# Expert rows gathered as 64 tokens by two picks, with their sums on the two column halves of TensorE's array

## The reference

```python
def peer_sublayer(h, g_ffn, w_peer_q, keys_1, keys_2, peer_u, peer_v):
    x = rmsnorm(h, g_ffn).reshape(-1, shape[-1])
...
    v1, i1 = lax.top_k(s1, PEER_TOPK)
    v2, i2 = lax.top_k(s2, PEER_TOPK)
    cand = (v1[..., :, None] + v2[..., None, :]).reshape(T, PEER_HEADS, PEER_TOPK * PEER_TOPK)
    sc, ci = lax.top_k(cand, PEER_TOPK)
...
    eidx = (e1 * PEER_NKEYS + e2).reshape(T, PEER_HEADS * PEER_TOPK)
    gates = jax.nn.softmax(sc, axis=-1).reshape(T, PEER_HEADS * PEER_TOPK).astype(x.dtype)
...
    def block(args):
        xt, it, gt = args
        act = jax.nn.gelu(jnp.einsum('td,tkd->tk', xt, peer_u[it]), approximate=False)
        return jnp.einsum('tk,tkd->td', gt * act, peer_v[it])
```

## Time and profile before

| | us |
|---|---|
| median of 3 runs | 2607.19 |
| lowest, highest | 2602.67, 2608.74 |
| span of the profiled execution | 2607.3 |
| first fetch issued | 661.6 |
| last product of the gather (`Y`) starts | 2033.7 |
| PE, DVE, ACT, POOL busy | 2152.8, 1647.3, 1003.4, 702.4 |
| bytes moved by the gather's queue | 536.90 MB |

### The profile page before, as it was taken

How to read it: one execution, slowest core, us unless ns; L and a number is a source line. 1 busy time by engine, 2 the same in 40 slices (tenths; PEclk the granted TensorE clock), 3 DMA queues, 4 the chain that set the end, 5 groups by cost and what they waited for, 6 DMA issues and landing times. The chain is left out here.

```text
span 2607.3 us, 25567 instructions
## 1 busy us (share of the span) xinstructions
PE 2152.8 (83%) x8090; PEld 1334.7 (51%) x8090; DVE 1647.3 (63%) x3381; ACT 1003.4 (38%) x2477; POOL 702.4 (27%) x610
## 2 busy tenths in 40 slices
PE   6999978897878687877868887676777787899998
PEld 6778855676423232322324453232333474788877
DVE  5674266535888988878456776656766555555534
ACT  3213345323443343333334344435533455433322
POOL 0120031000444354443434454444444100000000
PEclk8999988998999899898989999787988897999999
DMA  7664200211899999999999999999999433222222
GB/s 243 218 208 113 67 5 26 77 61 75 340 419 420 400 403 420 396 420 398 415 380 415 414 414 411 420 370 359 420 419 420 159 92 122 91 97 97 80 81 97
DMA packets 142827, 683.18 MB, mean 262 GB/s; under 512 B 19648, under 2 KB 36320, under 8 KB 74224
## 3 DMA queue, kind: packets, MB, share of 16 engines
q0 software_dynamic: 73728, 536.90, 50.3%
q1 hardware_dynamic: 68976, 144.78, 17.0%
HBM read 679.50 MB, written 2.10 MB: 261 GB/s over the span
## 5 line engine op out<-in xcount | busy, mean ns | idle before, releaser
L2483 PE MATMUL peer_Y<-peer_w,peer_diag 128*128 128x512 f32 x1784 | 902.5, 645 | 242.2 <-ACT peer_diag L2469 215.2
L2428 POOL DMA_INDIRECT peer_w<-in_peer_uv,peer_eidx x510 | 606.4, 1189 | 703.7 <-PE peer_Y L2483 465.8
L2437 DVE CUSTOM_DVE_ANT_0 peer_w<-peer_w,peer_xtok 128x1024 f32<-128x1024 f32 x510 | 617.7, 1222 | 198.1 <-DMA peer_w<-in_peer_uv,peer_eidx 195.3
L2483 PEld LDWEIGHTS peer_Y<-peer_w,peer_diag 128*128 128x128 f32 x1784 | 337.8, 202 | 753.2 <-ACT peer_diag L2469 443.7
L2461 ACT ACTIVATE peer_gel<-peer_dots 128x1 f32<-128x1 f32 x512 | 103.8, 203 | 721.8 <-DVE peer_dots L2437 721.5
L2469 ACT ACTIVATE peer_diag<-all_ident,peer_a 128x128 f32<-128x128 f32 x448 | 179.8, 401 | 18.1 <-PE peer_Y L2483 3.6
L2463 ACT ACTIVATE peer_a<-peer_gel,peer_gates 128x1 f32<-128x1 f32 x512 | 150.8, 294 | 16.6
L2992 PE MATMUL m_acc<-m2x_hs,m2x_cut 128*128 128x512 f32 (+1 forms) x384 | 143.7, 374 | 6.4 <-PEq L123 3.7
L2993 PE MATMUL m_acc<-m2x_hs,m2x_cut 128*128 128x512 f32 (+1 forms) x384 | 143.3, 373 | 0.0
L2994 PE MATMUL m_acc<-m2x_hs,m2x_cut 128*128 128x512 f32 (+1 forms) x384 | 143.2, 373 | 0.0
L1293 ACT ACTIVATE p_cut<-m1h_raw 128x512 fp32r<-128x512 f32 (+2 forms) x96 | 58.2, 609 | 202.1 <-PE p_acc L1240 119.3
(11 more groups left out here) (518 smaller groups left out, 3731.2 us busy)
## 6 DMA issues: line engine op xcount, KB each, us to landing
m_gates<-in_w_ada SPq DMA_DIRECT2D x48, 512.0 KB, 4.3
m2x_raw<-in_w_up SPq DMA_DIRECT2D x22, 1024.0 KB, 4.8
m1h_raw<-in_w_in SPq DMA_DIRECT2D x80, 256.0 KB, 3.1
m20h_raw<-in_w_in SPq DMA_DIRECT2D x48, 256.0 KB, 7.3
m22h_raw<-in_w_in SPq DMA_DIRECT2D x48, 256.0 KB, 2.8
m_down_ring<-in_w_down SPq DMA_DIRECT2D x22, 512.0 KB, 3.4
m_out_ring<-in_w_out SPq DMA_DIRECT2D x16, 512.0 KB, 7.8
peer_w<-in_peer_uv,peer_eidx POOLq DMA_INDIRECT x510, 16.7
```

Of the source, the lines that this page charges most:

```text
L2428: pool.indirect_dma_start(self.slot(n).rearrange("p c n -> p (c n)"), None, self.uv_dram, bass.IndirectOffsetOnAxis(self.col(self.eidx, n) ...
L2437: dve.tensor_tensor_reduce(u, u, self.xtok[:, n // PICKS, :], 1.0, 0.0, ALU.mult, ALU.add, self.col(self.dots, n)).then_inc(self.dotted, 1)
L2483: ins = pe.matmul(self.Y[:, h, :], self.diag[:, i % self.RD, :], self.slot(n)[:, 1, h * BANK:(h + 1) * BANK], start=(k == 0), stop=(i == l ...
```

## The change

A transfer now carries two picks for 64 tokens instead of one pick for 128. Item n = 128 t + k with q = k mod 2 belongs to the token half q of tile t (tokens 64 q to 64 q + 63): partitions 0 to 63 hold one pick of each of these tokens and partitions 64 to 127 another. It is still 128 rows of 8 KB, and still 512 items. To bring the picks into that layout stage 21 of the top-k writes `eidx` and `gates` in eight operations on 64 partitions instead of two on 128.

The dot product needs each half tile of tokens twice, in both partition halves. So `norm_rows` stores the normed tiles to HBM (`x_normed`) and `load_rows` brings back half tiles, each with two copies (`xrep`, two buffers of 1024 columns, one for each q). The two of tile 0 are loaded on SP inside `norm_rows`; those of tile t + 1 on ACT, behind the dot products of items 126 and 127 of tile t. The normed tiles no longer stay in SBUF.

Items are handled in pairs (m = n // 2). ACT makes one Gelu of two columns per pair. DVE makes for each item of the pair a 128x64 matrix `Z` (two stacked 64x64 identities times Gelu times gate), at the start of step 2m + 2, ahead of that step's dot product. PE multiplies with 64 weight columns: q = 0 gives rows 0 to 63 of `Y`, q = 1 rows 64 to 127, four matmuls in the order q = 0, 1, 0, 1. All items go to PE; DVE's own additions (L2446), the gate product and the diagonals on ACT are gone. A buffer is free when its pair is used.

```diff
--- before.py
+++ after.py
-def load_early(sp, sem, early):
...
+def issue_early(sp, sem, early):
...
+def await_early(sp, sem, early):
...
@@ norm_rows, SP
-            load_early(sp, early_landed, early)
+            issue_early(sp, early_landed, early)
+            if gather is not None:
+                for t in range(NT):
+                    sp.wait_ge(scaled, t + 1)
+                    sp.dma_start(gather.x_dram[t * P:(t + 1) * P, :], xn[:, t, :]).then_inc(gather.stored, 16)
+                    if t == 0:
+                        sp.wait_ge(gather.stored, 16)
+                        for q in range(2):
+                            gather.load_rows(sp, 0, q)
+                sp.wait_ge(gather.stored, 16 * NT)
+            await_early(sp, early_landed, early)
@@ TopK.vector, stage 21
-            dve.scalar_tensor_tensor(self.eidx[:, t, ks], e[:, 0, ks], float(NKEYS), e[:, 1, ks], ALU.mult, ALU.add)
-            ins = dve.tensor_tensor(self.gates[:, t, ks].rearrange("p (h k) -> p h k", h=n), self.ex[:, hs], bc(self.rden[:, hs], 2, K), ALU.mult)
+            for q in range(2):
+                rows = slice(64 * q, 64 * q + 64)
+                for c in range(2):
+                    at, own = slice(64 * c, 64 * c + 64), slice(h0 * K + c, (h0 + n) * K, 2)
+                    items = slice(h0 * K + q, (h0 + n) * K, 2)
+                    dve.scalar_tensor_tensor(self.eidx[at, t, items], e[rows, 0, own], float(NKEYS), e[rows, 1, own], ALU.mult, ALU.add)
+                    ins = dve.tensor_tensor(self.gates[at, t, items].rearrange("p (h k) -> p h k", h=n), self.ex[rows, hs, c:K:2],
...
@@ Gather
+    def load_rows(self, engine, t, q):
+
+        rows = self.x_dram[t * P + 64 * q:t * P + 64 * q + 64, :]
+        engine.dma_start(self.xrep[:, q, :], bc(rows, 0, 2)).then_inc(self.x_landed[q], 16)
...
-        self.fetch(pool, min(self.N, step + self.RW - 3))
+        limit = self.fetched
+        while limit < self.N and (limit < self.RW + len(self.lent) or (limit - self.RW) // self.BATCH * self.BATCH + self.BATCH < step):
+            limit += 1
+        self.fetch(pool, limit)
...
-                pool.wait_ge(*self.consumed(n - self.RW))
+                pool.wait_ge(self.used, (n - self.RW) // self.BATCH + 1)
...
     def vector(self, dve, s):
+        m = s // 2 - 1
+        if s % 2 == 0 and 0 <= m < self.N // 2:
+            dve.wait_ge(self.gelued, m + 1)
+            if m >= 2:
+                dve.wait_ge(self.used, m - 1)
+            for q in range(2):
+                n = 2 * m + q
+                dve.scalar_tensor_tensor(self.Z[:, m % 2, q, :], self.halves[:], self.col(self.gel, n), self.col(self.gates, n).to_broadcast([P, 64]), ALU.mult, ALU.mult).then_inc(self.spread, 1)
         n = s
         if n < self.N:
+            t, q = n // PICKS, n % 2
+            if n % PICKS < 2:
+                dve.wait_ge(self.x_landed[q], 16 * (t + 1))
             dve.wait_ge(*self.landing(n))
             u = self.slot(n)[:, 0, :]
-            dve.tensor_tensor_reduce(u, u, self.xtok[:, n // PICKS, :], 1.0, 0.0,
-                                     ALU.mult, ALU.add, self.col(self.dots, n)).then_inc(self.dotted, 1)
-        n = s - 2
-        if 0 <= n < self.N and not self.on_pe(n):
...
-            dve.scalar_tensor_tensor(y, self.slot(n)[:, 1, :], self.col(self.a, n), y, ALU.mult, ALU.add).then_inc(self.folded, 1)
+            dve.tensor_tensor_reduce(u, u, self.xrep[:, q, :], 1.0, 0.0, ALU.mult, ALU.add, self.col(self.dots, n)).then_inc(self.dotted, 1)
...
@@ Gather.scalar
+        t, k = divmod(n, PICKS)
+        if k >= PICKS - 2 and t + 1 < NT:
+            act.wait_ge(self.stored, 16 * NT)
+            act.wait_ge(self.dotted, n + 1)
+            self.load_rows(act, t + 1, n % 2)
+        if n % 2:
+            act.wait_ge(self.dotted, n + 1)
+            act.activation(self.col(self.gel, n - 1, 2), self.col(self.dots, n - 1, 2), ACT.Gelu).then_inc(self.gelued, 1)
@@ Gather.tensor
+        pe.wait_ge(self.spread, 2 * m + 2)
...
         for h in range(2):
-            ins = pe.matmul(self.Y[:, h, :], self.diag[:, i % self.RD, :], self.slot(n)[:, 1, h * BANK:(h + 1) * BANK],
-                            start=(k == 0), stop=(i == last))
+            for q in range(self.BATCH):
+                ins = pe.matmul(self.Y[64 * q:64 * q + 64, h, :], self.Z[:, m % 2, q, :], self.slot(first + q)[:, 1, h * BANK:(h + 1) * BANK],
+                                start=(k == 0), stop=(k == PICKS - self.BATCH))
```

More of the change, by code:

```diff
@@ L93, in shape_constants @@
     out["c_ident"] = np.eye(P, dtype=np.float32)
+    out["c_halves"] = np.tile(np.eye(64, dtype=np.float32), (2, 1))
     out["c_iota"] = np.tile(np.arange(P, dtype=np.float32), (P, 1))
@@ L238, in load_early @@
 def load_early(sp, sem, early):
[L240 to L244, removed]
+    issue_early(sp, sem, early)
+    await_early(sp, sem, early)
+def issue_early(sp, sem, early):
+    for e in early:
+        for dst, src in e.loads:
+            sp.dma_start(dst, src).then_inc(sem, 16)
+def await_early(sp, sem, early):
+    n = sum(len(e.loads) for e in early)
+    if n:
+        sp.wait_ge(sem, 16 * n)
 class Side:
@@ L650, in _, with norm_rows @@
             side.tensor(pe, len(tiles) - 1)
-def norm_rows(nc, name, consts, resid, hs, gain_dram, meta=None, load=None, early=(), keep=None, stats=None):
+def norm_rows(nc, name, consts, resid, hs, gain_dram, meta=None, load=None, early=(), stats=None, gather=None):
     ident, half = consts["ident"], consts["half"]
@@ L722, in scale @@
                 dve.wait_ge(*((roots, i + 1) if stats is None else (stats.roots, i + 1)))
-                if i >= 2 and keep is None:
+                if i >= 2 and gather is None:
                     dve.wait_ge(turned, i - 1)
@@ L2474, in tensor @@
+        if s % self.BATCH or not 0 <= m < self.N // self.BATCH:
             return
-        t, k = divmod(n, PICKS)
-        i = self.products(n)
-        pe.wait_ge(self.diaged, i + 1)
-        pe.wait_ge(*self.landing(n))
+        first = m * self.BATCH
+        t, k = divmod(first, PICKS)
+        pe.wait_ge(self.spread, 2 * m + 2)
         if k == 0 and t >= 1:
             pe.wait_ge(self.added, 2 * t)
-        last = self.products((t + 1) * PICKS) - 1
+        for q in range(self.BATCH):
+            pe.wait_ge(*self.landing(first + q))
@@ L2482, in tensor, with pick @@
         for h in range(2):
-            ins = pe.matmul(self.Y[:, h, :], self.diag[:, i % self.RD, :], self.slot(n)[:, 1, h * BANK:(h + 1) * BANK],
-                            start=(k == 0), stop=(i == last))
+            for q in range(self.BATCH):
+                ins = pe.matmul(self.Y[64 * q:64 * q + 64, h, :], self.Z[:, m % 2, q, :], self.slot(first + q)[:, 1, h * BANK:(h + 1) * BANK],
+                                start=(k == 0), stop=(k == PICKS - self.BATCH))
         ins.then_inc(self.used, 1)
-def pick(nc, gather, top, qT, keys, mod, rows, steps):
-    ident = gather.consts["ident"]
+def pick(nc, gather, ident, top, qT, keys, mod, rows, steps):
@@ L2616, in peer_and_front @@
                 xs = ph2.line("xs", [P, 2, KD, SEQ])
-                norm_rows(nc, "n2", consts, resid, xs, d["g_ffn_row"], early=[ring, tables], keep=xtok, stats=stats)
+                norm_rows(nc, "n2", consts, resid, xs, d["g_ffn_row"], early=[ring, tables], stats=stats, gather=gather)
                 Phase.gathering = True
@@ L2621, in peer_and_front @@
             gather.open()
-            pick(nc, gather, top, qT, tables["keys"], mod, kept.rows, STANDALONE)
+            pick(nc, gather, consts["ident"], top, qT, tables["keys"], mod, kept.rows, STANDALONE)
         pacer = Pacer(gather, STANDALONE)
-        second_front(nc, consts, resid, mod, d, kept, HALF, xtok[:, 0:2, :], qT[:].rearrange("p h q -> p (h q)"), pacer)
+        space = ph.sb("space", [P, 2, D])
+        second_front(nc, consts, resid, mod, d, kept, HALF, space[:], qT[:].rearrange("p h q -> p (h q)"), pacer)
         finish_gather(nc, gather, pacer.next)
```

65 lines of the change are left out of this document (22 added, 43 removed).

## The result

| | us |
|---|---|
| before, median | 2607.47 (2602.67 to 2608.74) |
| after, median of 4 runs | 2747.98 (2746.0 to 2751.88) |
| ratio | 1.0537, 95% interval 1.0515 to 1.0559 |
| forecast, with its range | 2742 (2625 to 2785) |
| span of the profiled execution before, after | 2607.3, 2747.2 |

The account below looks back on a forecast made before the run. The DMA engines were taken to bound the gather; 28 + 1 + 31 + 38 + 30 + 15 - 8 = 135 us on a span of 2607.3 gave 2742 us, range 2625 to 2785.

Parts of the forecast that it names:

- rival C: PE's column halves don't overlap at 512 columns: up to 30 us on top of the forecast, 2770 us; chance 0.03.
- +28: In norm_rows, two x loads on two DMA engines delay the stores and the barrier, from 616.2 to 644: 28 us.
- 31, 38 and 30: Losses in us at the ends of tiles 0, 1 and 2, from x loads on two DMA engines.
- the extra 7 for the barrier after tile 1: About half of the 13.6 us of barrier and load before second_front's norm shows, on top of 31.
- The sign that I named for it: Long top-k stretches after steps 87, 143 and 211 would show POOL idle over 12 us.
- -8: Gain from fetches running further at phase ends and shorter PE bursts in m20l: 8 us, between 0 and 20.
- +15: Three long top-k stretches, 5 us each, because the pair's Z stands behind 9 us of top-k operations.
- Rival A: The x loads spread over all 16 engines: 28 us slower, 2635 us; chance 0.20.
- dots wait some 4 us, inside the cushion: At tile ends with loads over 16 engines, dot products wait some 4 us, covered by queued fetches.
- +8 for `norm_rows`: With loads over 16 engines, the barrier in norm_rows comes at 624, 8 us later.
- Rival B: Faster: PE causes the lost DMA time in the gather and 30 us come back, 2592 us; chance 0.06.
- the 49 lost us: DMA time lost over the 1373 us gather, at a mean of 405 against 420 GB/s: 49 us.

Follow-up runs that it names:

- e1: The changed kernel with every xrep load written as two DMAs of 64 rows, so over all 16 engines: 2658.07 us, ratio 1.0195.
- e4: The changed kernel with xrep loads over 16 engines and the pair's Z made ahead of the long top-k operations at steps 87, 143, 211: 2655.58 us, ratio 1.0184.
- e10: The kernel before with one added wait on POOL, so that buffers are freed in pairs: 2630.16 us, ratio 1.0079.
- e11: The changed kernel with xrep loads over 16 engines, Z on ACT, no barrier wait for the last stores, nothing in pairs: 2630.59 us, ratio 1.0080.
- e7: The kernel before with fetches allowed to run one item further: 2613.20 us, ratio 1.0021.
- e9: The changed kernel with xrep loads over 16 engines but none at tile ends (tiles 1 to 3 take tile 0's tokens, output wrong): 2632.31 us, ratio 1.0079.
- e6: The changed kernel with xrep loads over 16 engines and PE's four matmuls of a pair in the order q = 0, 0, 1, 1: 2655.97 us, one run.

## Why the prediction was right, and where it was not

**What bounds the kernel.** Right: PE's busy time fell by 223 us (2152.8 to 1929.9), ACT's by 382 (1003.4 to 621.9), and none of it showed. The mean over the gather fell from 405 to 376 GB/s.

**Products and matrices.** Two lines of the page's fifth part:

```profile
L2513 PE MATMUL peer_Y<-peer_w,peer_Z 128*64 128x512 f32 x2040 | 663.6, 790 | 568.3 <-DVE peer_Z L2471 442.3
...
L2471 DVE SCALAR_TENSOR_TENSOR peer_Z<-peer_halves,peer_gel,peer_gates 128x64 f32<-128x64 f32 x512 | 121.7, 279 | 32.8 <-ACT peer_gel L2498 31.4
```

Eight records of a pair took 1.94 us at full clock (forecast 2.1 to 2.4) and 3.4 to 3.7 at half (4.3): the halves overlap fully, rival C is out. The mean of 790 ns in the line is that of single records, which overlap. A `Z` took 0.24 us of DVE, not 0.15.

**The x loads.** Right in cause and size. The Trainium skill (DMA: Bandwidth & Descriptors, "Rules for kernel authors") says that a leading broadcast of c copies confines a DMA to at most c engines; the trace agrees (a DMA share of 0.13 at 53 GB/s, two of 16 engines; and e1). In `norm_rows` I had the last store landing at 642.4; two engines still work between 642 and 644 (share 0.10) and `query_cut` starts at 644.4: +28.2 for +28, and 28.3 counted from the phase's first load. At the tile ends 31, 38 and 30 became 37, 32 and 32. The sum, 99, measured 101, but the extra 7 for the barrier after tile 1 isn't there: the 13.6 us of norm and barrier there seem to lie in the gap that the loads leave anyway. DVE's wait for the norm's `m20n_gain`, 12.3 us before, is 5.5 in after, which fits; no run isolates it.

**The long stretches.** Measured by the table, items 88 to 120 cost after 4.2 us, 136 to 208 nothing and 208 to 248 3.2: 7 instead of 15. The cause that I gave (`Z` behind the long operations) fell with e4. The sign that I named for it, POOL idle over 12 us there, isn't seen either: its longest idle stretches behind steps 87, 143 and 211 are 8.2, 8.2 and 10.1 us. What costs there is most likely that buffers come free in twos (e10 loses 3 to 4 us at each; e11 gets some of it back).

**What comes back.** I had -8 and e7 shows no gain from a longer reach. From item 264 to 376 after loses 5.0 us more, and from 392 to 504 it regains 4.4: about nothing instead of -8. This and the over-priced +15 cancel, and that is luck: 135 forecast, 140 measured, with two terms wrong by about 8 us each in opposite directions. The 5 us that are missing lie in small pieces, 2.5 before item 88, for which I had no term, and 2.4 at the tile ends.

**Rival A** had the right question and the wrong price: 28 us, where e1 has 50. Its step "dots wait some 4 us, inside the cushion" failed: the wait is 7.3 us for the first load and more for the second, POOL idles 15.6 us, and the loads at tile ends cost 22 to 26 us (e9) where A had 12. Its +8 for `norm_rows` measures 12. So of the 50 us some 12 lie at the barrier and 22 to 26 are the loads at tile ends. For the rest, 12 to 16, A had +15 - 8, and the pairs account for it, but not exactly: they cost 17 to 20 us where they were added (e10) or taken away (e11), while e9, which has them, needs only 9.5 us more than before for its dot products. From item 376 on e9 regains 7 us and e10 1, so the change gives something back there; what, no run isolates.

**Rival B** asked whether the 49 lost us would come back with a faster PE. They didn't: even e9, with PE relieved and no loads at the tile ends, needs 9.5 us more than before for its dot products. So what was lost there did not wait for the length of a product.

## What to carry to other kernels

A kernel that goes at the pace of its DMA engines must be asked first what a change does to the spread of its transfers over the engines: 4 MB of side loads on two of sixteen engines cost 90 us more than the same bytes as two DMAs per load, an edit of a few lines. Here the broadcast over the two partition halves looked like an ordinary load of 128 partitions. Where a ring of buffers feeds such a kernel, free each buffer by itself: one added wait that frees them in twos cost 20 us at nine buffers (e10). And price a small load beside such a stream by the time that one takes to land there, not by its bytes: 256 KB took 10.9 us beside the gather and 4.5 in `norm_rows` (medians of e1), where the bytes are 0.6 at 420 GB/s. Last, when two executions are compared stage by stage, count from an instant right before the edit: `norm_rows` started at 594.4 us in one execution and at 607.2 in another.

## What the runs showed of the hardware

**A product of 64 columns is as long as one of 128.** In e11 an item's two products of 64 weight columns stand alone; the windows of the same stretch are of e11 and of e1:

```profile
837.45 1.93 PE L2507 MATMUL peer_Y<-peer_w,peer_Z 128*64 128x512 f32 x4 [0.56 <-ACT peer_Z L2494]
```

```profile
835.00:860.00 25.00, 18.19 (x38) 4.47 (x39) 21.11 (x62) 7.60 (x27) 11.28 (x10) 1.00 1.01 419
```

```profile
845.00:872.00 27.00, 14.46 (x40) 3.27 (x40) 24.98 (x80) 1.02 (x5) 9.96 (x9) 0.76 1.01 420
```

Four records of 64 columns take 1.93 us, four of 128 took 1.98, and eight of 64 on both halves 1.94. The ends of records are modelled, but the fetches that they release agree: 2.21 us after the item's first record in e11 (839.66) and 2.22 after the pair's in e1. All the gain is overlap, and it comes without alternation too (e6).

**With less work PE had a lower clock.** With pairs PE is busy 14.5 of 27 us and the granted clock is 0.76, a mix of 2.4 and 1.2 GHz, so that some pairs take 1.94 us and others 3.4 to 3.7; with one item at a time it is busy 18.2 of 25 us at 1.00. Over the gather it was 0.92 before and 0.77 in after, of which little is due to the waits at tile ends: e9, without them, has 0.80, and e11 0.93. 256 pairs at 1.94 us would be 497 us of PE; they took 663.6. What the lower clock costs in time no run here shows.
